# Hidden activations of two MLPs stored in reverse token order and streamed backwards into TensorE

## The reference

```python
def squared_relu_mlp(u, w1, w2):
    return jnp.square(jax.nn.relu(u @ w1)) @ w2
...
h = h + squared_relu_mlp(rmsnorm(h, mlp_norm_g[layer]), mlp_w1[layer], mlp_w2[layer])
```

## Time and profile before

| | |
|---|---|
| three runs | 3262.06, 3251.28, 3255.86 us; median 3255.86 |
| profiled execution, span from first to last instruction | 3252.8 us |
| time of the profiled execution beside its span | none is listed; the span lies inside the range of the three runs, 3.1 us below their median |
| PE busy / PEld busy / DVE busy / ACT busy | 98% / 95% / 58% / 46% |
[...]

### The profile page before, as it was taken

The page is one execution under the profiler, slowest core; times in us unless marked ns, Lnnn a source line. Parts: engine busy times, 40 slices in busy tenths (PEclk is TensorE's granted clock), DMA queues, the critical chain, the costliest instruction groups (busy, mean ns, idle before and its releaser), DMA issues.

```text
span 3252.8 us, 59500 instructions
## 1 busy us (share of the span) xinstructions
PE 3191.9 (98%) x25757; PEld 3094.3 (95%) x25757; DVE 1885.6 (58%) x1694; ACT 1509.2 (46%) x1596; POOL 183.8 (6%) x164
## 2 busy tenths in 40 slices
PE   8999999999999999999999999999999999999998
PEld 7998889999789999999999999999988999999998
DVE  7755554766777555544444445555776555545454
ACT  5455543655556654443433334433454434434343
POOL 2140000000021200000000000100001000000001
PEclk9999999999999999999999999999999999999999
DMA  8564443889764455555655555555434666666664
GB/s 257 158 186 132 143 137 123 278 287 292 272 224 155 140 162 176 174 177 180 180 174 177 181 177 175 184 170 177 149 128 144 194 194 193 195 192 193 192 194 147
DMA packets 552496, 598.39 MB, mean 184 GB/s; under 512 B 9920, under 2 KB 531136, under 8 KB 552320
## 3 DMA queue, kind: packets, MB, share of 16 engines
q1 hardware_dynamic: 550416, 589.18, 57.7%
q0 software_dynamic: 1760, 6.59, 0.7%
q10 hardware_dynamic: 144, 0.01, 0.0%
HBM read 593.64 MB, written 2.10 MB: 183 GB/s over the span
## 4 chain that ended last, share of the span: by engine, by line
PE 85%; DVE 7%; ACT 3%; DMA 2%; issue 1%; SPq 1%; POOL 0%; DVEq 0%; ACTq 0%; POOLq 0%
PE acc L620 23%; PE acc L625 23%; PE acc L623 23%; DVE low L1904 2%; ACT high L1320 2%; PE psx L1164 1%; PE acc L1066 1%; PE acc L1068 1%; PE acc L1067 1%; DMA raw<-in_w_expert_up 1%; PE acc L1149 1%; PE psx L1149 1%; PE psx L1147 1%; PE acc L1147 1%; PE acc L1148 1%
## 5 line engine op out<-in xcount | busy, mean ns | idle before, releaser
L620 PE MATMUL acc<-gh,high 128*128 128x256 f32 (+1 forms) x4416 | 900.6, 285 | 15.3 <-DVE low L1939 8.7
L623 PE MATMUL acc<-gl,high 128*128 128x256 f32 (+1 forms) x4416 | 887.0, 283 | 0.0
L625 PE MATMUL acc<-gh,low 128*128 128x256 f32 (+1 forms) x4416 | 886.6, 282 | 0.0
L2189 DVE TENSOR_TENSOR low<-raw,high 128x2048 fp32r<-128x2048 f32 x264 | 605.2, 2293 | 401.1 <-ACT high L1556 401.1
L1904 DVE TENSOR_TENSOR low<-raw,high 128x2048 fp32r<-128x2048 f32 x261 | 606.9, 2329 | 334.3 <-ACT high L1320 333.9
L1556 ACT ACTIVATE high<-raw 128x2048 fp32r<-128x2048 f32 x264 | 505.4, 1914 | 494.4 <-DMA raw<-in_mlp_w 486.6
L620 PEld LDWEIGHTS acc<-gh,high 128*128 128x128 f32 x4416 | 681.5, 189 | 26.6 <-issue 16.4
L625 PEld LDWEIGHTS acc<-gh,low 128*128 128x128 f32 x4416 | 679.4, 189 | 0.0
L623 PEld LDWEIGHTS acc<-gl,high 128*128 128x128 f32 x4416 | 677.7, 189 | 0.0
L1320 ACT ACTIVATE high<-raw 128x2048 fp32r<-128x2048 f32 x261 | 498.4, 1913 | 316.6 <-DMA raw<-in_w_kv 66.5
L625 PE MATMUL acc<-fh,low 128*128 128x272 f32 (+1 forms) x2048 | 408.8, 281 | 0.0
(11 more groups left out here) (465 smaller groups left out, 3558.5 us busy)
## 6 DMA issues: line engine op xcount, KB each, us to landing
raw<-in_mlp_w SPq DMA_DIRECT2D x256, 1024.0 KB, 5.4
raw<-in_w_in SPq DMA_DIRECT2D x59, 1024.0 KB, 5.2
raw<-in_a_w_in SPq DMA_DIRECT2D x40, 1024.0 KB, 5.1
raw<-in_w_expert_up SPq DMA_DIRECT2D x32, 1024.0 KB, 6.0
raw<-in_w_expert_down SPq DMA_DIRECT2D x32, 1024.0 KB, 5.2
raw<-in_w_kv SPq DMA_DIRECT2D x32, 1024.0 KB, 5.5
raw<-in_w_expert_gate SPq DMA_DIRECT2D x28, 1024.0 KB, 5.8
raw<-in_a_w_out SPq DMA_DIRECT2D x20, 1024.0 KB, 5.0
```

The costliest lines, as they stand in the source:

```text
L620: pe.matmul(o[n], hw[:, k, c[n]], h, start=first and not (packed and n), stop=False, skip_group_check=packed)
L623: pe.matmul(o[n], hw[:, k, c[n]], l, start=False, stop=False, skip_group_check=packed)
L625: m = pe.matmul(o[n], lw[:, k, c[n]], h, start=False, stop=last, skip_group_check=packed)
L2189: dve.tensor_tensor(tile(low, k, k % SLOTS), tile(raw, k, k % SLOTS), tile(high, k, k % SLOTS).bitcast(F32), ALU.subtract)\
```

## The change

A helper `backwards` returns the same tile with its last dimension read from the last element to the first. It is used at three places: ACT's copy into `ah` and DVE's difference into `al` read `zb` backwards (so the hidden values are stored with the last token first), and the second layer's matmuls read `ah` and `al` backwards (so the tokens come out in their usual order in the accumulators). The order of instructions on each engine, their number and all waits stay the same.

```diff
+        def backwards(x):
+
+            *outer, (step, n) = x.ap
+            return bass.AP(x.tensor, x.offset + (n - 1) * step, [*outer, (-step, n)])
...
                     pairs_stage(name, 8, 2, lambda kt: h[:, kt, 0:T], lambda kt: l[:, kt, 0:T],
                                 first=need_g(8 * split) if c == 0 else None,
                                 hook=(lambda: stats(r, T)) if c == 0 else None, b_off=16 * c, u_off=32 * c)
-                    pairs_stage(name, 8, 2, lambda kt: ah[:, kt, :], lambda kt: al[:, kt, :],
+                    pairs_stage(name, 8, 2, lambda kt: backwards(ah[:, kt, :]), lambda kt: backwards(al[:, kt, :]),
                                 first=need_hid(base + 8 * c), b_off=16 * c + 8, u_off=32 * c + 16)
...
                             act.activation(z, z, ACT.Square).then_inc(hid_sq, 1)
                             act.wait_ge(hid_sq, i * 2 + (base + 8 * c + pr + 1))
-                            act.activation(ah[:, ds(i * 4 + 2 * pr, 2), :], z, ACT.Copy).then_inc(hid_hi, 1)
+                            act.activation(ah[:, ds(i * 4 + 2 * pr, 2), :], backwards(z), ACT.Copy).then_inc(hid_hi, 1)
...
                             t = ds(i * 4 + 2 * pr, 2)
-                            dve.tensor_tensor(al[:, t, :], z, ah[:, t, :].bitcast(F32), ALU.subtract).then_inc(hid_lo, 1)
+                            dve.tensor_tensor(al[:, t, :], backwards(z), ah[:, t, :].bitcast(F32), ALU.subtract).then_inc(hid_lo, 1)
```

## The result

The changed kernel takes 3276.73 us (median of 5 runs, 3272.22 to 3278.37); beside it the kernel before took 3256.51 us (5 runs, 3251.28 to 3262.06). The ratio is 1.0057, with a 95% interval of 1.0043 to 1.0071: 20 us slower. The profiled executions say the same, 3273.3 against 3252.8 us of span, with a mean granted clock of 0.998 and 0.997.

A forecast was written before the change was run, and what follows sets the result against it. The prediction took the pace of TensorE's matmuls to bound the kernel. Its terms, 0 + 0 on a span of 3252.8 us, plus 3.1 us by which the runs' median exceeds it, gave 3256 us, range 3222 to 3300 us.

The forecast's parts named there:

- no visible change: Whole kernel: likeliest case, 3246 to 3266 us around 3256 us, chance 0.38.
- a change of pace beyond 1.6 ns: Second-layer matmuls: such a change per matmul (9.8 us), with the first layer unchanged, would make the forecast wrong.
- worse fit: Rival, second-layer matmuls: 64-byte relation of activations and weights given up, 5.5 ns each, 34 us, 3290 us; chance 0.17.
- What bounds the kernel: MLPs: only the pace of matmuls counts; each nanosecond on the second layer's 6144 matmuls is 6.1 us.
- ACT's copy and DVE's difference: 64 of each before the second layer: at most doubled, 0.65 and 0.71 us more per pair; costed at nothing.
- The cover: Chunk's end: last hidden values needed only after 84 second-layer matmuls, giving 7 us of cover for 1.4 us.
- The backward matmuls: Second layer's 6144 matmuls reading backwards: taken as zero, between 43 us less and 688 us more.
- the 688 us: Second-layer matmuls: the slow end of the bound on the backward read, 688 us more.
- The end of 43 us less: Second-layer matmuls: the most gained down to the 111 ns weight load, 37 us in mlp0 and 6 us in mlp1.
- the 119 ns row: Sort's 256-column matmuls at another relation of the streams: 119 against 113 ns, nearest neighbour, 5.5 ns a matmul.
- The two streams fit better: Rival, second-layer matmuls: half of the bound won, 22 us, 3234 us; more matmuls with 272 tokens; chance 0.30.
- Backward streaming is slow by itself: Rival, second-layer matmuls: some 340 and 315 matmuls in the stretches that held 651 and 620; chance 0.15.

The follow-up runs named there:

- e3: Changed kernel split by chunk: chunks 0 and 1 only ACT and DVE read backwards, chunks 2 and 3 only TensorE does; 3268.71 us.
- e2: Kernel before, all read forward, hidden tiles shifted 0, 64, 128, 192 bytes in chunks 0 to 3 of each MLP; 3277.22 us.
- e5: Kernel before, forward, weight tiles from mlp0 on 64 bytes further on, hidden tiles shifted 0, 64, 128, 192 bytes by chunk; 3313.17 us (3256.97 before).
- e6: Kernel before, all read forward, hidden tiles shifted 16, 32, 48, 96 bytes in chunks 0 to 3; 3284.73 us.
- e9: Kernel before, forward, weights 64 bytes further on, hidden tiles 60, 56, 68, 72: differences of −4, −8, +4, +8 bytes; 3325.11 us (3256.87 before).
- e8: Second-layer weight loads held at one address; chunks 0 and 2 forward, 1 and 3 backward, chunks 2 and 3 shifted 128 bytes; 3275.16 us.
- e1: Changed kernel, hidden tiles shifted 0, 64, 128, 192 bytes in chunks 0 to 3 of each MLP; 3285.72 us (3255.15 before).
- e4: Changed kernel, backward reads, hidden tiles shifted 4, 8, 16, 32 bytes in chunks 0 to 3; 3292.19 us.
- e7: Changed kernel, backward reads, hidden tiles shifted 80, 96, 160, 176 bytes in mlp0 and as in e1 in mlp1; 3291.76 us.
- e10: The change in mlp0 alone, mlp1 as in the kernel before; 3261.96 us, ratio 1.0017.
- e11: The change in mlp1 alone, mlp0 as in the kernel before; 3272.72 us, ratio 1.0044.
- e12: Changed kernel with one short matmul of 16, 64, 144 or 208 columns ahead of each second layer in chunks 0 to 3; 3282.12 us.

## Why the prediction was right or wrong, by its steps

**The forecast.** The measured 3276.73 us lies inside the range (3222 to 3300 us), but the likeliest case, no visible change (3246 to 3266 us, chance 0.38), did not come, and by the prediction's own sign, a change of pace beyond 1.6 ns, that forecast is wrong: 1.67 and 4.45 ns. What came is *worse fit*, which had 0.17. The range held because it left room for that rival, not because the loss was foreseen: as far as the forecast's own reasoning goes, that is luck.

**What bounds the kernel: right.** Only the pace of matmuls moved the end: 18.8 of 20.5 us of span come from it, and 6.1 us per nanosecond is the right exchange: half of 6144 matmuls at 1.67 ns and half at 4.45 give 3072 × 6.12 ns = 18.8 us.

**ACT's copy and DVE's difference: right.** They were bounded by twice their length and costed at nothing; they did not even grow, since the medians stayed at 646 and 709 ns, e3 shows nothing in the chunks that only write in reverse, and DVE waits for ACT's copy as long as in the earlier trace rows:

```profile
DVE fl L2591 <- ACT fh L1778: 102.8, 64, 1.7
```

The cover held: after the chunk's last accumulators the pair is done 3.1 us later in both kernels (1444.44 to 1447.54 in the earlier trace rows; here 1445.10 to 1447.47 + 0.73), well ahead of the 84 matmuls. DVE's timeline after:

```profile
1445.10 0.72 DVE L2587 SCALAR_TENSOR_TENSOR zb<-acc,inv 128x544 f32<-128x544 f32 x1 [2.26 <-PE acc L630]
1447.47 0.73 DVE L2591 TENSOR_TENSOR fl<-zb,fh 128x544 f32 x1 [1.65 <-ACT fh L1778]
```

**The backward matmuls: the step that failed.** "I take zero for this term", between −43 and +688 us; it is +18.8. No run shows the 688 us: that end was the author's estimate, and in its place the runs showed a loss of 1.67 and 4.45 ns a matmul. The end of 43 us less held, and the reasoning towards the right neighbour was there: the 119 ns row is at the same width and says 5.5 ns for a place given up, and the runs found 4.45 with 256 tokens and 1.67 with 272. What went wrong is the sign. I held a loss and a gain to be alike, so that zero stood in the middle. But of the two paces at 256 columns that I had read, 113 ns in the MLPs is 2 ns above the weight load's 111, and 119 ns belongs to another relation. A stream that stands 2 ns above its floor can lose from a change of relation and hardly gain. The runs show the same one-sidedness: of 30 forward stages with moving weights at another difference (6 in e2, 8 in e5 with its first layers counted once a width, 8 in e6, 8 in e9), 29 were slower, by 1.7 to 8.9 ns, and one, with 272 tokens in e9, was equal. The sentence "`mlp1` is at this floor nearly now" held the answer for 256 columns and was used for the lower bound only. For 272 it does not do: `mlp0` stood 12 ns above the 111 and still nothing gained. What holds for both widths is that the kernel before stood at the best of all the forward places tried; that constants of its own (`PHASE`, `PHASE_AT`) put it there was a sign of this that the prediction did not weigh.

**One word.** By e9 a difference of one word costs 6.7 to 8.9 ns with 256 tokens, and the change itself, for which the prediction took zero, cost 4.45 ns there and 1.67 with 272.

**The rivals.** *The two streams fit better* is refuted: it expected more matmuls with 272 tokens, and 642 stood there for 651. Nor did any run win some of the 12 ns between 111 and 123: no MLP stage at 272 columns fell below 123.33, and with standing weights the pace is 124.44 in either direction (e8). *The two streams fit worse* came true in sign, and at 18.8 us for its 34. Its count with 256 tokens was near (590, measured 597), with 272 too pessimistic (620, measured 642); with 272 tokens the loss was the smaller (1.67 against 4.45 ns a matmul), and no run shows why. As a cause it is borne out for 272 columns in that the direction costs nothing once the weights stand still (e8), though none of twelve backward places with moving weights gave 123.33 back (e1, e4, e7). For 256 it is open: place does cost 3.4 to 8.9 ns there when reading forward (e2, e5, e6, e9), but with the weights standing still the two directions differ by 4.4, which e8 leaves undecided between direction and the second pace. *Backward streaming is slow by itself*, at about half speed (some 340 and 315 matmuls, where 642 and 597 stood), is refuted: at the change's own place a backward matmul loses 1.4% at 272 columns and 3.9% at 256.

**What stays open.** Shown is that TensorE's backward read makes the loss (e3, e10, e11); not shown is why. Open is, above all, why no backward stream of 256 columns reached 113.33 ns, in e1, e4, e7, e8 and e12, at eight places, with moving and standing weights and, with moving weights, four entries. What in the memory makes the difference modulo 256 count was not measured; the runs give its effect only.

## What to carry to other kernels

Where a stream of matmuls sets the time, read its pace as a stretch divided by its starts, and compare it with the nearest floor of the trace (here 111 ns) before costing a change of addresses: close to the floor such a change has little to win (here 2 of 113 ns) and some nanoseconds times thousands to lose (4.45 × 3072, 13.6 us), and a layout that somebody has placed with constants may stand at its best place already. Treat the addresses of the moving operand and of the weights as a pair, and after any edit to layout, pitch or direction look at the pace again, since the busy shares can stay as they were (PE's was 98% before and after). Reading backwards on ACT and DVE cost nothing here (medians of 646 and 709 ns before and after).

## What was not expected of the hardware

- The pace of matmuls depends on the difference of the two operands' addresses modulo 256 bytes, to the single word: 113.33 to 122.22 ns at 256 columns, 123.33 to 126.67 at 272, all forward (e2, e5, e6, e9). That the period is 256 rests on one difference: −64 bytes (e5) has the paces of 192 (e2). Some of these paces may be the second of the two below.
- A stream can keep either of two paces at one pair of addresses. The unchanged forward first layer of `mlp1` ran at 113.35 ns in some chunks and at 117.78 in others (about 90.45 us in e1, e4, e6, e7, e8 and e12), for all its 768 matmuls, and e7 repeated e1's chunks exactly. Only what ran before it differs there; what in it picks the pace is not shown.
- One word of shift backward cost 272 columns 3.3 ns, to 128.33 (e4), more than the change itself did (1.67).
